# 80 adaLN weight blocks move from TensorE matmuls to row products with summed output on VectorE

## The reference

```python
mod = silu(c) @ ada_w[l] + ada_b[l]          # per layer 6 x 1024 numbers, for c_ctx (context) and c (latent)
shift1, scale1, gate1, shift2, scale2, gate2 = split(mod, 6)
xn = rmsnorm(x) * (1 + scale1) + shift1
y  = even_mixer(xn)  # layer 0: 4 mLSTM heads, 4 retention heads
y  = odd_mixer(xn)   # layer 1: 4 gated linear attention heads
x  = x + gate1 * rmsnorm(y)
xn = rmsnorm(x) * (1 + scale2) + shift2
a, v = split(xn @ ffn_w_in, 2)               # 2 x 2816 features
y  = (gelu(conv3x3(a) + b) * v) @ ffn_w_out
x  = x + gate2 * rmsnorm(y)
```

## Time and profile before

| | |
|---|---|
| median of 3 runs | 3712.99 us (3712.21 to 3724.08) |
| profiled execution | 3716.3 us, its span (first to last instruction) 3714.4 us |
| TensorE busy | 3374.4 us, 91% |
| VectorE busy | 1938.8 us, 52% |
| ScalarE busy | 797.1 us, 21% |
| GpSimd busy | 1003.5 us, 27% |
| mean granted TensorE clock | 0.939 of full |
| adaLN matmuls of the 80 blocks | 1280 records |

### The profile page before, as it was taken

The page is one execution under the profiler, slowest core; times in us unless marked ns, Lnnn a source line. Parts: engine busy times, 40 slices in busy tenths (PEclk is TensorE's granted clock), DMA queues, the critical chain, the costliest instruction groups (busy, mean ns, idle before and its releaser), DMA issues. The chain is left out here.

```text
span 3714.4 us, 49369 instructions
## 1 busy us (share of the span) xinstructions
PE 3374.4 (91%) x19579; PEld 3288.1 (89%) x19579; DVE 1938.8 (52%) x2395; ACT 797.1 (21%) x1557; POOL 1003.5 (27%) x435
## 2 busy tenths in 40 slices
PE   8899998987989999999997988888698999999996
PEld 8788888986989999999997877777698999999995
DVE  1333332222276666566666233434327777777775
ACT  1433332112041111111112332333204111111110
POOL 1112111112213333333330211111122344344440
PEclk8899999988999999999998988989899999999998
DMA  4111111112321111111122101101231111111112
GB/s 165 42 47 55 56 55 61 54 62 97 105 72 57 68 68 67 69 68 56 56 96 80 33 26 39 41 24 43 75 113 47 38 42 40 45 40 41 44 40 102
DMA packets 86089, 225.58 MB, mean 61 GB/s; under 512 B 8000, under 2 KB 45120, under 8 KB 85872
## 3 DMA queue, kind: packets, MB, share of 16 engines
q1 hardware_dynamic: 44064, 163.16, 12.7%
q10 hardware_dynamic: 41936, 61.17, 4.8%
HBM read 193.89 MB, written 30.41 MB: 60 GB/s over the span
## 5 line engine op out<-in xcount | busy, mean ns | idle before, releaser
L717 PE MATMUL bank<-xh,wh 128*128 128x384 f32 x3888 | 1357.3, 349 | 81.0 <-DVE xl L2090 35.3
L717 PE MATMUL bank<-xl,wh 128*128 128x384 f32 x3888 | 1332.0, 343 | 0.0
L717 PE MATMUL bank<-xh,wl 128*128 128x384 f32 x3888 | 1329.5, 342 | 0.0
L698 POOL TENSOR_TENSOR wh<-raw,ones 128x1024 fp32r<-128x1024 f32 x206 | 424.3, 2060 | 2611.8 <-PE bank L717 1584.6
L717 PEld LDWEIGHTS bank<-xh,wh 128*128 128x128 f32 x3888 | 756.0, 194 | 110.2 <-issue 78.3
L717 PEld LDWEIGHTS bank<-xl,wh 128*128 128x128 f32 x3888 | 756.9, 195 | 0.5
L717 PEld LDWEIGHTS bank<-xh,wl 128*128 128x128 f32 x3888 | 754.8, 194 | 0.0
L2111 DVE SCALAR_TENSOR_TENSOR cc<-pad,cw,cc 128x1024 f32<-128x1024 f32 x352 | 606.7, 1723 | 12.6
L700 POOL TENSOR_TENSOR wl<-raw,wh 128x1024 fp32r<-128x1024 f32 x206 | 574.0, 2786 | 16.2
L717 PE MATMUL bank<-hh,wh 128*128 128x384 f32 x1056 | 362.4, 343 | 34.0 <-DVE y L2155 14.9
L2141 DVE TENSOR_TENSOR y<-y,bank 128x384 f32<-128x384 f32 x480 | 263.2, 553 | 205.5 <-PE bank L717 202.4
(11 more groups left out here) (233 smaller groups left out, 2750.8 us busy)
## 6 DMA issues: line engine op xcount, KB each, us to landing
raw<-in_w SPq DMA_DIRECT2D x206, 512.0 KB, 3.3
ada_w<-in_ada SPq DMA_DIRECT2D x80, 512.0 KB, 3.6
residual_scratch<-y ACTq DMA_DIRECT2D x9, 1536.0 KB, 6.0
xg<-residual_scratch ACTq DMA_DIRECT2D x9, 1536.0 KB, 8.4
xr<-mixer_scratch ACTq DMA_DIRECT2D x16, 576.0 KB, 3.8
front<-in_ada SPq DMA_DIRECT2D x16, 512.0 KB, 7.9
y<-in_x SPq DMA_DIRECT2D x1, 4608.0 KB, 19.7
mixer_scratch<-hout ACTq DMA_DIRECT2D x24, 192.0 KB, 1.9
```

Source lines behind the costliest of these rows:

```text
L698: nc.gpsimd.tensor_tensor(wh[s][:, :], raw[s][:, :], ones[:, 0:1].broadcast_to([128, 1024]), ALU.mult).then_inc(w_hi[s], 1)
L717: return nc.tensor.matmul(out, lhsT, rhs, start=start, stop=stop)
```

## The change

The 80 blocks are no longer matmuls. VectorE multiplies a block, now laid out with its 128 output columns on the partitions and the 1024 inputs along the row, with the conditioning vector (`condb`, broadcast to all partitions) and sums the row (`tensor_tensor_reduce`): one instruction per block and conditioning vector, 160 in all. `ada_w` becomes two buffers. `condb` is loaded once (1 MB) and put through Silu by ScalarE. In the heads all four blocks of a conditioning stand behind `states_even`; in the feed-forward turns two stand inside `down()` (one in each half, ahead of its seventh tile) and two at the turn's end. SP's order of loads changes with it.

```diff
-        ada_w = sb("ada_w", [128, 1024])
+        ada_w = [sb(f"ada_w{s}", [128, 1024]) for s in range(2)]
+        condb = sb("condb", [128, 2, 1024])
+        products = sb("products", [128, 1024])
+        fresh = sb("fresh", [128, 4, 2])
...
-            def ada(n):
-
-                if seen.count.get(ada_used.name, 0):
-                    sp.wait_ge(ada_used, seen.before(ada_used))
-                seen.next(ada_used)
-                sp.dma_start(ada_w[:, :], a["ada"][n]).then_inc(ada_loaded, 16)
+            def ada(n, s):
+
+                sp.wait_ge(ada_used, seen.next(ada_used))
+                sp.dma_start(ada_w[s][:, :], a["ada"][n]).then_inc(ada_loaded[s], 16)
...
-            stream("first", 1, "wwawawaa")
-            stream("head0", 1, "wawawawa")
-            stream("heads", 6, "wawawawa")
+            sp.dma_start(condb[:, :, :], a["condb"]).then_inc(condb_loaded, 16)
+            stream("first", 1, "ww")
+            for s in range(2):
+                sp.dma_start(ada_w[s][:, :], a["ada"][ADA_FRONT + s]).then_inc(ada_loaded[s], 16)
+            state["ada"] += 2
+            stream("first", 1, "ww")
+            stream("head0", 1, "wwaaaaww")
+            stream("heads", 6, "wwaaaaww")
             stream("last", 1, "waaaa")
-            stream("out0", 4, "ww")
-            stream("ffn_a", 1, "wawawawa")
-            stream("ffn_b", FP - 1, "wawawawaww")
-            stream("ffn_c", 1, "ww")
+            stream("out0", 1, "wwaaaa")
+            stream("out0", 3, "ww")
+            stream("ffn_a", 1, "wwww")
+            stream("ffn_b", FP - 1, "wwawawaaww")
+            stream("ffn_c", 1, "wwaa")
...
-            def ada(j):
-
-                if j == 0:
-                    claim(4)
-                pe.wait_ge(ada_loaded, n.next(ada_loaded, 16))
-                for k in range(KT):
-                    last = mm(mb[4][:, 2 * j:2 * j + 2], ada_w[:, k * 128:(k + 1) * 128], cond[:, k, :], k == 0, k == KT - 1)
-                last.then_inc(ada_used, 1)
...
+            act.wait_ge(condb_loaded, 16)
+            fn(condb[:, :, :], condb[:, :, :], ACT.Silu).then_inc(condb_ready, 1)
...
-            def conditioning(column):
-
-                dve.wait_ge(ada_used, n.next(ada_used, 4))
-                give(v.tensor_tensor(mod[:, bass.ds(column, 4), :], mb[4][:, 0:8].rearrange("p (c g) -> p c g", g=2),
-                                     b3(ada_b[:, bass.ds(column, 4)], 2), ALU.add), mb_free[4])
+            def ada(j):
+
+                s = j % 2
+                dve.wait_ge(ada_loaded[s], n.next(ada_loaded[s], 16))
+                for g in range(2):
+                    link(v.tensor_tensor_reduce(products[:, :], ada_w[s][:, :], condb[:, g, :], 1.0, 0.0, ALU.mult, ALU.add,
+                                                fresh[:, j, g:g + 1]), ada_used if g else dve_order)
+
+            def conditioning(column, blocks_=range(4)):
+
+                for j in blocks_:
+                    ada(j)
+                link(v.tensor_tensor(mod[:, bass.ds(column, 4), :], fresh[:, :, :],
+                                     b3(ada_b[:, bass.ds(column, 4)], 2), ALU.add))
...
                 states_even(mlstm)
+                conditioning(ada_turn)
...
                 head_norm(o, num[:, :, 1, 0:CH], CH)
-                conditioning(ada_turn)
...
                     for m in range(4):
+                        if with_ada and m == 2:
+                            ada(half)
...
                 if column is not None:
-                    conditioning(column)
+                    conditioning(column, (2, 3) if with_down else range(4))
```

More of the change, by code:

```diff
@@ L163 @@
               'w_used1': 3},
- 'dve.mlstm': {'ada_used': 4,
-               'dve_order': 32,
+ 'dve.mlstm': {'ada_loaded0': 32,
+               'ada_loaded1': 32,
+               'ada_used': 4,
+               'dve_order': 37,
                'e_masked': 6,
@@ L222 @@
              'z_logs': 2},
- 'dve.ret': {'ada_used': 4,
-             'dve_order': 18,
+ 'dve.ret': {'ada_loaded0': 32,
+             'ada_loaded1': 32,
+             'ada_used': 4,
+             'dve_order': 23,
              'front_done': 3,
@@ L277 @@
               'mb_free3': 7,
-              'mb_free4': 4,
+              'mb_free4': 3,
               'o_ready': 1,
@@ L546, in build @@
         w_used = [sem(f"w_used{s}") for s in range(2)]
-        ada_loaded, ada_used = sems("ada_loaded ada_used")
+        condb_loaded, condb_ready, ada_used = sems("condb_loaded condb_ready ada_used")
+        ada_loaded = [sem(f"ada_loaded{s}") for s in range(2)]
         la_free = sem("la_free")
@@ L624, in once @@
                         else:
-                            ada(turn * na + (a0 + c))
+                            ada(turn * na + (a0 + c), (a0 + c) % 2)
                             c += 1
@@ L941, in head_even @@
                     front_even(2, mlstm)
-                    for j in range(4):
-                        ada(j)
                     for t in range(8):
@@ L1133, in ffn @@
             def ffn(layer):
-                with_ada = layer == 0
-                if with_ada:
-                    ada(0)
                 for j in range(1, 4):
                     project_all(slot())
-                    if with_ada:
-                        ada(j)
                 with n.loop(pe, f"pe.ffn{layer}", FP - 1):
@@ L2127, in act_takes, with down @@
                     n.next(pj_full[c])
-            def down():
+            def down(with_ada):
                 for half in range(2):
@@ L2170, in pair @@
                 if with_down:
-                    down()
+                    down(column is not None)
                 else:
@@ L2339 @@
     arrays["cond"] = np.stack([np.asarray(c_ctx), np.asarray(c)[0]], 1).reshape(KT, 128, 2).transpose(1, 0, 2)
+    arrays["condb"] = np.broadcast_to(np.stack([np.asarray(c_ctx), np.asarray(c)[0]])[None], (128, 2, D))
     ada_w, ada_b = np.asarray(ada_w), np.asarray(ada_b)
@@ L2346 @@
                 at, j = mod_column(layer, part, k), 8 * part + k
-                ada[at] = by_features(ada_w[layer][:, 128 * j:128 * j + 128])
+                w = ada_w[layer][:, 128 * j:128 * j + 128]
+                ada[at] = by_features(w) if at < ADA_FRONT else w.T
                 bias[:, at] = ada_b[layer][128 * j:128 * j + 128]
```

35 lines of the change are left out of this document (11 added, 24 removed).

## The result

| | before | after |
|---|---|---|
| median | 3713.1 us (4 runs) | 3605.5 us (4 runs, 3602.0 to 3609.4) |
| ratio | | 0.970, 95% interval 0.9683 to 0.9717 |
| span of the profiled execution | 3714.4 us | 3607.7 us |
| mean granted TensorE clock | 0.939 | 0.940 |

The gain is 108 us; the forecast was 93, with a range of 3595 to 3650. Predicted 3620, measured 3605.

What follows compares the result with a forecast made beforehand. TensorE, busy 91% of the span and fully in feed-forward turns, was taken as the bound. Feed-forward 55, retention 27, mLSTM -6, last even head 14, start 3.5 sum to 93 us: 3620 us, own range 3595 to 3650.

Steps and rivals of the forecast that it cites:

- a forecast of -6: Four mLSTM heads, head 0 included: -1.5 us each, splits and the lower clock outweighing 3.5 us from removed blocks.
- 1.44 us was taken: VectorE's price per product: 1.26 us for the product, 0.15 for the read-out, 0.03 for the gap.
- The tap row: Profile row used to price a product: two SBUF tensors multiplied and added on VectorE, 1024 elements, 1.285 us.
- Rival 1: Each product's sum costs a second pass per element, 2.5 us a product: slower, 3742 us; chance 0.10.
- a forecast of 6.6: Nine steady feed-forward turns: 75.4 us instead of 82.0 each, 59 us in all.
- the 0.4 allowed: Loss allowed per steady feed-forward turn for VectorE's added products: 0.4 us.
- two pauses that four banks cover: Blocks inside down() stop VectorE's adds for 2.9 us, and 2.9 us is free in each half.
- +1, not +14: Feed-forward's start: late taps, TensorE standing about 10 us in the down projection with four banks full; +1 us.
- Forecast -5: Feed-forward's end: two blocks and mod, 5.9 us, between hl and the last down projection's first add; -5 us.
- forecast 9: Three retention heads: about 9 us each from removed blocks, a removed split wait and clock regained; 27 in all.
- the forecast mechanism: mLSTM heads: splits with loads on time meet VectorE's chain, 1.9 us in the front, 2 to 4 in the tail.
- Rival 2: Splits miss the mLSTM heads' VectorE chain: 3.5 + 1.5 us more per head, 3600 us; chance 0.08.

Runs made afterwards that it cites:

- run 2: Kernel after with every product issued twice (320 products, same result): 3815.4 us, ratio 1.0262.
- run 1: Kernel after with each of the 160 products replaced by a one-column memset, loads and their order kept: 3590.3 us, ratio 0.9663.
- run 3: Kernel after with all four blocks of a feed-forward turn at its end, none inside down(), SP's load order following: 3702.0 us, ratio 0.9960.
- run 10: As run 8, but with two weight loads ahead of the four adaLN loads in SP's order: 3599.0 us, ratio 0.9686.
- run 11: Kernel after with GpSimd splits held back in mLSTM heads, eight blocks in the output projection, none in the last turn, SP's order adapted: 3576.7 us, ratio 0.9618.
- run 4: Kernel before with two adaLN buffers and dynamic_dma_scratch_size=1024, blocks still on TensorE: 3699.0 us, ratio 0.9953.
- run 5: Kernel after with GpSimd splits held at two places per mLSTM head, until the head norm and until two fronts are done: 3596.0 us, ratio 0.9668.
- run 8: Kernel after with pair 0's four blocks moved into the even mixer's output projection, SP's order following: 3609.7 us, ratio 0.9709.

## Why the prediction was right, and where it was not

The forecast of 93 us is near the 107 us by which the profiled span fell, and most of it rests on the two stages that came as worked out, steady turns and retention heads. The nearness of the sum owes a little to luck: the mLSTM heads gained 4.0 us for a forecast of -6, the retention heads 4 more than forecast, and the feed-forward 3 to 4 less, which took back some of it.

**Price of a product.** 1.44 us was taken, 1.26 measured (pitch). The tap row was the right neighbour; the 0.15 for the read-out was too much, since it runs inside the product's end. Rival 1 (2.5 us) is refuted: two full fp32 SBUF tensors and a sum cost no more than the taps' 1.285 us without one. That rival's time was mis-sized, though: run 2 had such a price and came out near 3810, not 3742.

The rule of the Trainium skill, "Vector Engine (DVE) Microarchitecture Reference", "Points that are easy to get wrong", that a family of instructions with two SBUF sources that are not bf16 runs at half the throughput, does not hold here as the prediction read it, as twice the taps' time. The page names no rate that it halves, and the profile names the product `CUSTOM_DVE_ANT_0` and not `SCALAR_TENSOR_TENSOR` like the taps; `TENSOR_SCALAR`, with one such source of the same size, takes 0.75 us. So other readings of the rule stay open.

**Steady turns.** Right: 6.73 us each for a forecast of 6.6. Run 1 shows 0.2 us of loss, of the 0.4 allowed, at 1.26 us a product and not the 1.44 for which the room was worked out. The reason given, work that fits the idle ahead of the first tap and two pauses that four banks cover, is borne out by run 3, in which the same work without the spread, and with its order of loads, costs 9 us a turn.

**The first two turns.** The step that failed is "+1, not +14". Its mechanism was wrong: TensorE did not wait in `down()` with its banks full, as it does in run 10, but 3.67 us for v0's split and 9.98 us ahead of v1's projections, for ScalarE. Corrected for the place of the copy the stretch lost 4 us where it was to win 1. The prediction saw that the taps start late, and that v0's load is late; it did not follow the late taps through the GELU to the evacuation that TensorE needs.

**Feed-forward's end.** Forecast -5; run 1 gives 4.0 for the products of the last turn, and taking them away in run 11 brings 4.6.

**Retention heads.** 10.4 each, forecast 9. Both parts are there: in the second of them run 4 has 4.5 us from the loads and the clock behind them (3.7 was taken: the wait of 1.93 and 1.8 of clock), and the kernel after 5.8 us more from the blocks themselves (5.3 taken).

**mLSTM heads.** Heads 1 to 3 lost 0.2, 1.3 and 1.6 us (in other traces with this code up to 3.3, or nothing), by the forecast mechanism: run 4 makes it appear with no block removed, run 5 makes it go. Rival 2, splits that miss the chain, would gain 3.5 each; with the hold they gain 3.4 on average. The mis-sized term is head 0, counted with -1.5 and found at +7.1 (4.5 to 7.6 in the other runs with its code). Its squares are stretched like those of the others, but the stretched `tm` of heads 1 to 3 does not occur in it. Why it gains most or all of its blocks was not tested.

The Trainium skill, "SBUF — State Buffer", "Who interferes with whom", says that a VectorE instruction with two SBUF inputs and a GpSimd one that reads SBUF shut each other out; the trace agrees, and more plainly than before: the squares take 2.94 us with a split beside them and 1.36 without.

**Last even head, start.** 15.1 for 14, 3.6 for 3.5. Run 4 puts 8.8 of the 15.1 on loads. At the start it gained 4.5 us with all blocks still on TensorE, so the 3.6 can come from the loads alone; the prediction had counted removed blocks in it, and nothing shows that these gained there.

## What to carry to other kernels

- Price moved work by the stage: the same kind of instruction cost nothing that the trace shows in mLSTM and retention heads, 0.2 us in a steady turn, and 12.5 us in all at three places where the receiving engine was already late. A move is decided by where the receiver idles, so put such work there (here the output projection), and count also who waits behind it: taps, GELU, evacuation, TensorE.
- An in-order DMA queue that serves two consumers must have its entries in the order in which the buffers come free at that very place; an order that put adaLN loads ahead of weights stalled TensorE for 8 us in run 8, and two weight loads put first took that away.
- Earlier is not always better. A load on time let a GpSimd pass fall into VectorE's critical chain; one wait on the norm's semaphore was worth 4.4 us a head here, with the meeting in the next head's front gone as well.

## What was not expected of the hardware

- The product with sum (128x1024 fp32, two SBUF sources) takes 1.22 us and its accumulator's read-out 0.08, overlapping; in the run with 320 of them an undisturbed one keeps the same pitch of 1.26 to 1.27.
- A shift of less than 0.1 us decides whether a short VectorE instruction gets in ahead of a GpSimd pass or is stretched by it: 1.15 against 2.88 us for the two of `tm`. Three of eight products at the end of pair 0 took 2.9, 3.2 and 2.8 us beside two splits.
- A retention head that lost one wait of 1.8 us for a split (run 4, same matmuls) shows a granted clock of 0.98 instead of 0.94 and became 4.5 us shorter.
